# A third pair of steps by seven block products in four dense networks, and their weights in two transfers per step

## The reference, cut to what matters

```python
def swiglu(x, w_gate, w_up, w_down):
    return (jax.nn.silu(x @ w_gate) * (x @ w_up)) @ w_down
...
    h = x
    for layer in range(DEPTH_2):
        h = h + 0.5 * swiglu(rms_norm_2(h, ffn_norm[layer, 0]), ffn_w_gate[layer, 0], ffn_w_up[layer, 0], ffn_w_down[layer, 0])
        ...
        h = h + mixed.astype(h.dtype)
        h = h + 0.5 * swiglu(rms_norm_2(h, ffn_norm[layer, 1]), ffn_w_gate[layer, 1], ffn_w_up[layer, 1], ffn_w_down[layer, 1])
    return rms_norm_2(h, final_norm)
```

## Time and profile before

| | |
|---|---|
| time, median of 3 runs | 2255.48 us (2253.54 to 2258.27) |
| time of the profiled execution | 2258.86 us |
| its span, first to last instruction | 2257.0 us |
| PE busy | 2102.3 us (93%) |
| DVE busy | 1186.3 us (53%) |
| ACT busy | 807.4 us (36%) |
| mean granted clock of TensorE | 0.974 |
| transfers | 633.84 MB, mean 281 GB/s |

### The profile page before, as it was taken

How to read it: one execution, slowest core, us unless ns; L and a number is a source line. 1 busy time by engine, 2 the same in 40 slices (tenths; PEclk the granted TensorE clock), 3 DMA queues, 4 the chain that set the end, 5 groups by cost and what they waited for, 6 DMA issues and landing times.

```text
span 2257.0 us, 27346 instructions
## 1 busy us (share of the span) xinstructions
PE 2102.3 (93%) x10956; PEld 1286.6 (57%) x10956; DVE 1186.3 (53%) x1785; ACT 807.4 (36%) x1263; POOL 28.1 (1%) x38
## 2 busy tenths in 40 slices
PE   5999999999999899989868999999999999989998
PEld 3348743333333333333325878778877878867876
DVE  6975612222222212222215967768675976685966
ACT  6045321111111111111105544655545545375544
POOL 0000000000000000000000000100000000200000
PEclk9999889999999999999988999999999999999999
DMA  7773799999999999999996543444535253413442
GB/s 320 280 298 131 275 413 415 411 428 428 427 427 427 428 427 426 427 428 427 426 427 281 210 168 148 149 158 178 216 131 215 109 223 149 154 57 140 196 168 84
DMA packets 43507, 633.84 MB, mean 281 GB/s; under 512 B 5104, under 2 KB 5104, under 8 KB 6288
## 3 DMA queue, kind: packets, MB, share of 16 engines
q1 hardware_dynamic: 43376, 632.04, 67.6%
HBM read 630.97 MB, written 1.05 MB: 280 GB/s over the span
## 4 chain that ended last, share of the span: by engine, by line
PE 64%; DMA 20%; DVE 10%; ACT 4%; issue 1%; SPq 0%; DVEq 0%; ACTq 0%
DMA piece<-in_moe 15%; PE bank L2404 13%; PE bank L2281 10%; PE bank L2283 10%; PE bank L2282 10%; PE bank L2445 6%; DMA slot<-in_ffn 4%; DVE ffn_lo L2287 4%; PE bank L2379 3%; PE bank L2469 2%; PE bank L1034 2%; ACT ffn_hi L3240 1%; PE bank L2916 1%; PE bank L721 1%; PE bank L347 1%
## 5 line engine op out<-in xcount | busy, mean ns | idle before, releaser
L2404 PE MATMUL bank<-piece,xeT 128*64 128x512 f32 (+1 forms) x2304 | 450.0, 622 | 52.9 <-DMA piece<-in_moe 44.6
L2287 DVE TENSOR_TENSOR ffn_lo<-slot,ffn_hi 128x2048 fp32r<-128x2048 f32 x148 | 336.6, 2287 | 119.2 <-ACT ffn_hi L3240 118.8
L3240 ACT ACTIVATE ffn_hi<-slot 128x2048 fp32r<-128x2048 f32 x148 | 281.3, 1913 | 191.7 <-PE bank L2283 91.6
L2404 PEld LDWEIGHTS bank<-piece,xeT 128*64 128x64 f32 (+1 forms) x2304 | 135.4, 131 | 333.1 <-issue 311.0
L2525 DVE TENSOR_TENSOR hT<-hT,bank 128x512 f32<-128x512 f32 x144 | 92.2, 682 | 254.5 <-PE bank L2469 254.3
L2281 PE MATMUL bank<-ffn_hi,hT_hi 128*128 128x512 f32 x512 | 202.3, 395 | 0.0
L2283 PE MATMUL bank<-ffn_hi,hT_lo 128*128 128x512 f32 x512 | 199.7, 390 | 0.0
L2282 PE MATMUL bank<-ffn_lo,hT_hi 128*128 128x512 f32 x512 | 199.4, 389 | 0.0
L2574 DVE TENSOR_SCALAR work<-bank 128x256 f32<-128x256 f32 x60 | 25.5, 424 | 328.7 <-PE bank L2413 328.7
L2281 PE MATMUL bank<-ffn_hi,act_hi 128*128 128x512 f32 x288 | 114.8, 399 | 12.3 <-DVE act_lo L2287 12.3
L2283 PE MATMUL bank<-ffn_hi,act_lo 128*128 128x512 f32 x288 | 115.4, 401 | 0.0
(11 more groups left out here) (789 smaller groups left out, 3255.6 us busy)
## 6 DMA issues: line engine op xcount, KB each, us to landing
piece<-in_moe SPq DMA_DIRECT2D x190, 2048.0 KB, 26.3
slot<-in_ffn SPq DMA_DIRECT2D x44, 3072.0 KB, 10.6
slot<-in_ada SPq DMA_DIRECT2D x16, 1024.0 KB, 5.0
slot<-in_nsa_in SPq DMA_DIRECT2D x5, 2048.0 KB, 7.5
slot<-in_merge SPq DMA_DIRECT2D x3, 3072.0 KB, 12.6
slot<-in_ada SPq DMA_DIRECT2D x2, 3072.0 KB, 18.7
slot<-in_w_in SPq DMA_DIRECT2D x6, 1024.0 KB, 7.8
slot<-in_hy_in SPq DMA_DIRECT2D x3, 2048.0 KB, 7.9
```

What stands on the lines that cost most here:

```text
L2287: return dve.tensor_tensor(lo, x, hi.bitcast(F32), ALU.subtract)
L2404: mm = pe.matmul(bank[n * c:n * (c + 1), :], x[:, kt, :], w[i][:, at:at + 512], start=kt == 0, stop=False)
L3240: act.activation(k["ffn_hi"][:, room, :], ffn_plain(k, q, what), ACT.Copy).then_inc(s["ffn_down_hi"] if isinstance(what, int) else s["ffn_ ...
```

## The change

The third pair begins at step 2, the others at steps 5 and 8; steps 0, 1, 4, 7 and 10 stay plain. The queues of the three engines lose the plain steps 2 and 3 in front of the pairs and the plain step between them, so that steps 0 and 1 are followed by three times `pair`. `turned_low(m - 2)` and `turned_high(m - 2)` leave the pair's queues; `rows_whole`, `rows_sums` and `sums_low` come right behind `turned_low(0)`. `DOWN_ROOM`, the counts of the semaphores and the banks are set accordingly.

The weights of a step come in two transfers: gate and up (2 MB) and down (1 MB), in an order written out (`FFN_LOADS`). The first waits until the last block that reads the old gate and up weights of the slot has been split, the second until the old down weights have been. Two entries of the mixers wait for `ffn_down_lo` in addition, since they write to the end of a slot.

```diff
-FFN_PAIRS = (4, 8)
-FFN_DOWNS = (0, 1, 2, 3, 5, 4, 6, 7, 9, 8, 10)
+FFN_PAIRS = (2, 5, 8)
+FFN_DOWNS = (0, 1, 3, 2, 4, 6, 5, 7, 9, 8, 10)
...
-FFN_PARITY = {0: 0, 1: 1, 2: 0, 3: 1, 6: 1, 7: 0, 10: 0}
-DOWN_ROOM = {0: 3, 1: 2, 2: 3, 3: 3, 5: 2, 4: 3, 6: 2, 7: 2, 9: 3, 8: 2, 10: 3}
+FFN_PARITY = {0: 0, 1: 1, 4: 1, 7: 1, 10: 1}
+DOWN_ROOM = {0: 2, 1: 2, 3: 3, 2: 2, 4: 2, 6: 3, 5: 2, 7: 2, 9: 3, 8: 2, 10: 3}
...
     def ffn(q):
-        base = FFN_STEPS * q
-        for m in range(FFN_STEPS):
-            item(f"ffn{q}_{m}", ("ffn", q * FFN_STEPS + m), SLOT, (sig["ffn_down_lo"], base + FFN_POS[m] + 1))
+        nonlocal turn
+        slots = [(turn + m) % 3 for m in range(FFN_STEPS)]
+        turn += FFN_STEPS
+        for what, m in FFN_LOADS:
+            slot, src = slots[m], ("ffn", q * FFN_STEPS + m)
+            if what == "both":
+                landed[slot] += 16
+                plan[f"ffn{q}_{m}"] = Part(src, 0, 2 * PIECE, slot, 0, freed[slot], None, landed[slot])
+                order.append(plan[f"ffn{q}_{m}"])
+                freed[slot] = [(sig["ffn_w_lo"], FFN_COUNT * q + FFN_FORMS[FFN_LAST_FORM[m]])]
+            else:
+                at = ends_at[slot]
+                count[at] += 16
+                plan[f"down{q}_{m}"] = Part(src, 2 * PIECE, PIECE, slot, 2 * PIECE, ends_freed[slot], sems[at], count[at])
+                order.append(plan[f"down{q}_{m}"])
+                ends_freed[slot] = [(sig["ffn_down_lo"], FFN_STEPS * q + FFN_POS[m] + 1)]
...
-        if m + 3 < FFN_STEPS:
+        if m + 3 in FFN_PARITY:
...
+FFN_LAST_FORM = {m: (m, 1) for m in FFN_PARITY}
+for pair_first in FFN_PAIRS:
+    FFN_LAST_FORM[pair_first], FFN_LAST_FORM[pair_first + 1] = (pair_first, "A22 T4"), (pair_first, "S3 T3")
+FFN_LOADS = [(what, m) for what, group in (("both", (0, 1, 2)), ("down", (0, 1, 2))) for m in group]
+for step in (3, 4):
+    FFN_LOADS += [("both", step), ("down", step)]
+for step in (5, 8):
+    FFN_LOADS += [("both", step), ("both", step + 1), ("down", step + 1), ("both", step + 2), ("down", step), ("down", step + 2)]
...
         if base >= 1:
-            pe.wait_ge(s["act_ready"], base)
+            pe.wait_ge(s["act_ready"], base + 1)
...
         pair_sum(m, "T1")
-        turned_low(m - 2)
         pair_sum(m, "T3")
...
     turned_low(0)
-    low(2, 0)
-    low(1)
-    swiglu(1)
     rows_whole()
-    low(2, 1)
-    low(2)
-    turned_low(1)
-    low(3, 0)
     rows_sums()
-    swiglu(2)
-    low(3, 1)
     sums_low()
-    pair(4)
-    low(7, 0)
-    low(6)
-    swiglu(6)
-    low(7, 1)
-    pair(8)
+    for m in FFN_PAIRS:
+        pair(m)
     low(FFN_LAST)
...
-    high(2, 0)
-    high(1)
-    silu(1)
-    high(2, 1)
-    high(2)
-    turned_high(1)
-    high(3, 0)
-    silu(2)
-    high(3, 1)
     sums_high()
-    pair(4)
-    high(7, 0)
-    high(6)
-    silu(6)
-    high(7, 1)
-    pair(8)
+    for m in FFN_PAIRS:
+        pair(m)
...
-    return []
+    return [(s["ffn_down_lo"], FFN_STEPS - 1)]
...
-    return []
+    return [(s["ffn_down_lo"], 3 * FFN_STEPS - 1)]
```

More of the change, by code:

```diff
@@ L251, in plan_ring, with item @@
     before = list(order)
-    freed = [(sig["moe_gu"], len(MOE_PLAN[0].events))] * 3
+    freed = [[(sig["moe_gu"], len(MOE_PLAN[0].events))]] * 3
+    ends_freed = list(freed)
+    ends_at = ((0, 1), (0, 2), (2, 1))
     order.clear()
     turn = 0
-    def ffn(q):
-        base = FFN_STEPS * q
-        for m in range(FFN_STEPS):
-            item(f"ffn{q}_{m}", ("ffn", q * FFN_STEPS + m), SLOT, (sig["ffn_down_lo"], base + FFN_POS[m] + 1))
+    def item(name, src, width, done, slot=None):
+        nonlocal turn
+        if slot is None:
+            slot = turn % 3
+            turn += 1
+        landed[slot] += 16
+        plan[name] = Item(src, width, slot, freed[slot] + (ends_freed[slot] if width > 2 * PIECE else []), landed[slot])
+        order.append(plan[name])
+        freed[slot] = ends_freed[slot] = [done]
+    def ffn(q):
+        nonlocal turn
+        slots = [(turn + m) % 3 for m in range(FFN_STEPS)]
[3 more added lines that the diff above has]
+            if what == "both":
+                landed[slot] += 16
+                plan[f"ffn{q}_{m}"] = Part(src, 0, 2 * PIECE, slot, 0, freed[slot], None, landed[slot])
[7 more added lines that the diff above has]
+                ends_freed[slot] = [(sig["ffn_down_lo"], FFN_STEPS * q + FFN_POS[m] + 1)]
     ffn(0)
@@ L2833, in sum_count @@
 def sum_count(q, m, name):
-    return 12 * q + 4 + 4 * FFN_PAIRS.index(m) + PAIR_SUMS.index(name) + 1
+    return 16 * q + 4 + 4 * FFN_PAIRS.index(m) + PAIR_SUMS.index(name) + 1
 def kept_count(q, m, n):
-    return 8 * q + 4 + 2 * FFN_PAIRS.index(m) + n
+    return 10 * q + 4 + 2 * FFN_PAIRS.index(m) + n
 def joined_count(q, m, name):
-    return 13 * q + 1 + 6 * FFN_PAIRS.index(m) + PAIR_JOINS.index(name) + 1
+    return 19 * q + 1 + 6 * FFN_PAIRS.index(m) + PAIR_JOINS.index(name) + 1
 def pair_banks(k, q, m):
@@ L2967, in pair @@
         block(m, "A11 B11", a, True)
-        pe.wait_ge(s["ffn_joined"], 13 * q + 1)
+        pe.wait_ge(s["ffn_joined"], 19 * q + 1)
         block(m, "S4 B22", c, True)
@@ L3089, in rows_sums @@
         dve.tensor_tensor(room["S3"], a11, a21, ALU.subtract).then_inc(s["ffn_sum"], 1)
-        dve.wait_ge(s["ffn_sum"], 12 * q + 1)
+        dve.wait_ge(s["ffn_sum"], 16 * q + 1)
         dve.tensor_tensor(room["S2"], room["S1"], a11, ALU.subtract).then_inc(s["ffn_sum"], 1)
-        dve.wait_ge(s["ffn_sum"], 12 * q + 3)
+        dve.wait_ge(s["ffn_sum"], 16 * q + 3)
         dve.tensor_tensor(room["S4"], a12, room["S2"], ALU.subtract).then_inc(s["ffn_sum"], 1)
@@ L3096, in sums_low @@
         for n, name in enumerate(FFN_SUMS):
-            dve.wait_ge(s["ffn_kept"], 8 * q + n + 1)
+            dve.wait_ge(s["ffn_kept"], 10 * q + n + 1)
             ins = low_part(dve, sum_low(k, name), sum_room(k, name), sum_high(k, name))
@@ L3232, in ffn_form_high @@
     if isinstance(block, int) or block.split()[1][0] == "B":
-        it = k["plan"][f"ffn{q}_{m + 1 if block == 'S4 B22' else m}"]
-        act.wait_ge(k["landed"][it.slot], it.landed)
+        it = k["plan"][f"{'down' if isinstance(what, int) else 'ffn'}{q}_{m + 1 if block == 'S4 B22' else m}"]
+        act.wait_ge(k["landed"][it.slot] if it.sem is None else it.sem, it.landed)
     else:
@@ L3273, in sums_high @@
         for n, name in enumerate(FFN_SUMS):
-            act.wait_ge(s["ffn_sum"], 12 * q + n + 1)
+            act.wait_ge(s["ffn_sum"], 16 * q + n + 1)
             act.activation(sum_high(k, name), sum_room(k, name), ACT.Copy).then_inc(s["ffn_kept"], 1)
@@ L3283, in pair @@
         high(m, "A11 B11")
-        turned_high(m - 2)
         high(m, "S4 B22")
@@ L4390, in stream @@
                 for it in items:
-                    if it.free is not None:
-                        sp.wait_ge(*it.free)
+                    for sem_at in it.free if isinstance(it.free, list) else [it.free] if it.free is not None else []:
+                        sp.wait_ge(*sem_at)
                     name, i = it.src
                     if isinstance(it, Part):
-                        sp.dma_start(k["ring"][it.slot][:, it.at:it.at + it.width], src[name][i, :, it.lo:it.lo + it.width]).then_inc(it.sem, 16)
+                        sp.dma_start(k["ring"][it.slot][:, it.at:it.at + it.width], src[name][i, :, it.lo:it.lo + it.width]).then_inc(k["landed"][it.slot] if it.sem is None else it.sem, 16)
                         continue
```

## The result

The changed kernel takes 2320.12 us (median of 4 runs, 2317.97 to 2320.63) beside 2256.58 us for the kernel before (4 runs). The ratio is 1.0281, with a 95% interval of 1.0263 to 1.0299: slower by 63.5 us. 2308 us was forecast, with a range of 2286 to 2328. The profiled execution has a span of 2318.8 us; before it was 2257.0, so the two traces differ by 61.8 us.

The account below looks back on a forecast made before the run. TensorE was taken as full. Opening 47.0 plus pair to pair 29.4 less 37.8 saved gives +38.6 us; with 13.8 for the clock, +52 us on the median of 2255.5: 2308 us, range 2286 to 2328.

Parts of the forecast that it names:

- What goes away: Over four calls, blocks 10.9 us, PE's waits 16.9, slow clock 3.1 and late first weights 6.9: 37.8 us saved.
- The opening: From turned_low(0) to "S2 T2" of pair 2, DVE's queue takes 29.1 us; PE stands 11.8 us a call, 47 in all.
- the four waits named: PE's gaps in pair 2: 1.8 us before "A11 B11", 4 before "S4 B22", 2 before turn(1), 4 before "S2 T2".
- The one of 2 us before turn(1) and "A12 B21": In pair 2, PE waits about 2 us there for DVE, until +22.1 us after turned_low(0) starts.
- that slow stretch: Half clock behind the gap before "S4 B22" of pair 2: costs nothing more, DVE being late anyway.
- the 11 to 12 that I gave as a sign: Sign of being right: PE idle rows in pair 2, released by DVE, of 11 to 12 us a call.
- From pair to pair: "S2 T2" to the next pair's "S2 T2" takes 51.8 us; PE stands 3.7 before pairs 5 and 8, 29.4 in all.
- rival 3: The clock falls at each of the twelve gaps, by the dearest price seen: +71 us, 2326 us; chance 0.12.
- The clock: TensorE's slow clock behind gaps of about 4 us before "S2 T2": 12 x 1.15 = 13.8 us, bounds 0 and 32.
- 200 to 205 us as a sign: Sign of being right: dense networks last about 200 to 205 us in place of 190.
- DVE keeps up: Low parts come in time everywhere, DVE having 48 us to spare in 191: -37.8 us, 2218 us; chance 0.06.
- only the opening is late: The next pair's "A11 B11" doesn't wait in DVE's queue: +9 us, about 2269 with four clock drops; chance 0.07.

Follow-up runs that it names:

- the kernel with waits of 1.2 to 1.6 us: The changed kernel with the low part of down m-1 moved behind that of "A22 T4" in DVE's queue: 2267.03 us, ratio 1.0055.

## Why the prediction was right, point by point

**What goes away.** The block's 2.72 us, the DMA waits and the late weights at the end of the second call were forecast at 37.8 us, 26.9 of them from the transfers. The kernel with these alone gained 29.4, 2.5 more than the sum.

**The opening.** Forecast: "S2 T2" 29.1 us after turned_low(0) starts. Measured in the changed kernel: 1267.87 - 1238.80 = 29.07 us, and 29.08 in each of the other three networks; T1 at 1249.05 - 1238.80 = 10.25 (10.3). Of the four waits named, three came: 1.82 us (1.8 forecast), 3.64 (4) and 2.99 to 3.82 (4). The one of 2 us before turn(1) and "A12 B21" did not, but for 0.42 us once, because PE ran the block ahead of it at half clock. The forecast had put that slow stretch at no cost, which is so, but had not seen that it fills the next wait. So PE idles 7.7 to 9.7 us a call in the opening and not the 11 to 12 that I gave as a sign. Most of the rest it spends at half clock. The delay is as forecast, since DVE alone sets when "S2 T2" may start.

**From pair to pair.** Forecast 51.8 us and a gap of 3.7. Measured 51.83 us wherever the clock held (1639.06 to 1690.89, and in the kernel with matmuls in the gap), and gaps of 3.50. The step stood on one row of the kernel before, an idle row that cost nothing there. (One slip: eight times 51.82 - 48.11 is 29.7 us, where the prediction has 29.4; and its upper bound of 2328 is 2 us above its own sum for rival 3.)

**The clock** is the term that was mis-sized; it explains 10.6 of the 11.1 us by which the forecast of +52.4 was short of the measured 63.5. I took 12 gaps at a mean of 1.15 us, 13.8 us. The eight distances from pair to pair in the changed kernel add up to (1375.56 - 1267.87) + (1690.89 - 1585.71) + (1897.72 - 1788.99) + (2262.89 - 2155.11) = 429.4 us, 14.8 more than eight times 51.82. From the last "S2 T2" to the transposes that end the network 44.12 us were needed before. In the changed kernel these transposes stand in PE's timeline at:

```profile
1422.35 1.03 PE L612 MATMUL bank<-consts,x 128*128 128x128 f32 x8
...
1736.59 1.03 PE L612 MATMUL bank<-consts,x 128*128 128x128 f32 x8
...
1944.53 1.03 PE L612 MATMUL bank<-consts,x 128*128 128x128 f32 x8
```

That is 46.8, 45.7 and 46.8 us in the first three networks, and from the last one to the end of the span 55.9 in place of 53.3: 9.6 us. Together 24.4 us, 2.0 a gap. The clock fell behind eleven of the twelve gaps, where the kernel before had shown three of five; a fall cost 24.4 / 11 = 2.2 us, 5.7 / 3 = 1.9 before. So it was mostly the number of falls that I had too low. Why fewer followed before isn't shown: there a wait of 2.82 us was followed by one and a wait of 3.26 was not. It was the third rival's case but for one gap, at 2.2 us in place of 2.7. With it the sum is 38.6 + 24.4 = 63.0 us; the traces differ by 61.8, the medians by 63.5.

The networks are 207 to 209 us long, where I had given 200 to 205 as a sign: that number leaves too little room for the slow clock. That the result lies within the range, 12 us above the likeliest time, is due to its upper bound, which allowed for slow clock at every gap.

The page "TensorE: Matmul & The Clock Gate" of the Trainium skill, section "HAM oscillation — how this bites in real kernels", has the rule that recurring waits pay the change of clock every time. The trace of the changed kernel agrees with it in eleven of its twelve waits before "S2 T2"; in the kernel with waits of 1.2 to 1.6 us no trace of such a price is left.

**The rivals.** That DVE keeps up was wrong by the profile, and its reason, a busy share of three quarters, was the trap: DVE is still idle for 47 of 209 us in the first network of the changed kernel, and PE waits for it. The rival "only the opening is late" came true when the rooms were changed: it forecast 2269, the kernel took 2272. DVE's price by the page "VectorE: DVE Perf Modes" of the Trainium skill, section "The TRN2 errata — SBUF-src ops pay a fixed extra latency per instruction", is 2.29 us for 2048 columns, which agrees with the duration of one instruction. In the queue they follow each other at 2.2 (1300.19 to 1302.40), and a chain shows that the distance counts: from T1 to "S2 T2" the opening took 1267.87 - 1249.05 = 18.82 us, 18.83 by the distances, about 0.7 more by the durations.

## What to carry to other kernels

Work that an algorithm takes from the bound engine and puts on another one must fit where it falls, not on average: add up the second engine's queue between the two points at which the first waits for it. A row in which an engine idles at no cost, because nothing follows, shows what the same wait will cost in an order in which something does follow. And a change of two halves should be timed as two: here one gained 29 us, and the other lost 93 on top of it.

## What the runs showed of the hardware

Waits of PE of 3.0 to 3.8 us in front of "S2 T2" were followed by a stretch at half clock in eleven of twelve cases in the changed kernel. It was the same in the other kernels that have such waits: eleven of twelve with the sums of rows moved up, three of four with the other rooms, twelve of twelve with whole steps loaded, 37 of 40 in all. Waits of 2.8 to 4.0 us before the change were followed by one in three of five cases, waits of 1.2 to 1.6 us in none of twelve.

That is no safe bound: the wait of 1.8 us before "A11 B11" of pair 2 was followed by one too, in the third network of the changed kernel but in none of its other three (windows view), and in 5 of 20 cases over the five kernels with such a wait:

```profile
1770.50:1775.40 4.90, 4.49 (x12) 3.18 (x12) 4.90 (x3) 3.92 (x3) 0.00 (x0) 0.65 0.00 0
```

Each fall before "S2 T2" cost about 2 us of PE's time, more than half of the gap ahead of it. Twelve matmuls whose results nobody reads, in each of the twelve gaps, saved 28 us. That PE may win time by useless work I hadn't expected in such a size.
